# Differential mixer: each normalized output is transposed five steps behind its scores in place of four

## The reference

```
for blk in range(8):                       # 128 queries each, chunk-causal
    sc = einsum('bqhmd,bkhmd->bhmqk', q[blk], k[:qe]) * 64**-0.5   # 4 heads, 2 maps m
    sc = where(allowed, sc + bias, NEG_INF)
    pr = softmax(sc)
    a  = pr[:, :, 0] - lam * pr[:, :, 1]
    outs.append(einsum('bhqk,bkhe->bqhe', a, v[:qe]))              # 128 wide
o = rms_norm(concat(outs), subln_g) * (1 - lambda_init)
h = h + concat([oa, ob]) @ w_out           # oa: the sliding-window mixer
```

## Time and profile before

| | us |
|---|---|
| median of 3 runs | 1261.01 |
| lowest, highest | 1259.12, 1261.21 |
| the profiled execution | 1262.01 |
| its span | 1259.9 |
| PE busy in the span | 1219.5 |

### The profile page before, as it was taken

The page is one execution under the profiler, slowest core; times in us unless marked ns, Lnnn a source line. Parts: engine busy times, 40 slices in busy tenths (PEclk is TensorE's granted clock), DMA queues, the critical chain, the costliest instruction groups (busy, mean ns, idle before and its releaser), DMA issues.

```text
span 1259.9 us, 17110 instructions
## 1 busy us (share of the span) xinstructions
PE 1219.5 (97%) x6167; PEld 1004.0 (80%) x6167; DVE 868.3 (69%) x1510; ACT 517.3 (41%) x1042; POOL 248.5 (20%) x291
## 2 busy tenths in 40 slices
PE   8999999999789999999999999999999999999997
PEld 7997787887667787888888888888888888888885
DVE  5423786777886466887787777877677898964442
ACT  4311664665664224433333333333344444643321
POOL 0000000354454122232323323223120000000000
PEclk9999999999899999999999999999999999999998
DMA  7464233112833411333332323223398533620101
GB/s 210 91 89 87 51 85 84 31 43 72 219 124 61 141 50 59 101 110 99 112 98 85 125 88 122 84 84 125 135 326 317 174 94 104 222 67 25 43 34 50
DMA packets 128668, 136.07 MB, mean 108 GB/s; under 512 B 15570, under 2 KB 93130, under 8 KB 128522
## 3 DMA queue, kind: packets, MB, share of 16 engines
q1 hardware_dynamic: 128586, 135.00, 35.6%
HBM read 96.77 MB, written 37.22 MB: 106 GB/s over the span
## 4 chain that ended last, share of the span: by engine, by line
PE 63%; issue 2%; DVE 2%; DMA 1%; SPq 0%; ACT 0%; POOL 0%; POOLq 0%; DVEq 0%
PE ps L1687 62%; PE ps L1693 1%; DMA act_t<-mix_a 1%; DVE xs L1453 0%; PE ps L1927 0%; DVE h L1448 0%; DVE conv L1392 0%; SPq L479 0%; POOL stat L678 0%; ACT xs L787 0%; DVE act_t L1167 0%; PE ps L2077 0%; DVE gel L1680 0%; DVE h L1669 0%; DVE conv L1666 0%
## 5 line engine op out<-in xcount | busy, mean ns | idle before, releaser
L1687 PE MATMUL ps<-act_t,wbuf 128*128 128x512 f32 x1200 | 290.0, 398 | 2.9 <-DVE wbuf L1167 2.9
L1687 PEld LDWEIGHTS ps<-act_t,wbuf 128*128 128x128 f32 x1200 | 226.7, 189 | 57.8 <-issue 3.3
L1687 PE MATMUL ps<-wbuf 128*128 128x512 f32 x912 | 215.5, 391 | 0.0
L1687 PEld LDWEIGHTS ps<-wbuf 128*128 128x128 f32 x912 | 170.6, 188 | 36.2
L1687 PE MATMUL ps<-act_t,wq 128*128 128x512 f32 x624 | 155.7, 402 | 3.6 <-DVE wq L1169 2.8
L1687 PEld LDWEIGHTS ps<-act_t,wq 128*128 128x128 f32 x624 | 114.6, 188 | 33.5 <-issue 7.4
L678 POOL TENSOR_TENSOR stat<-stat 128x1 f32<-128x1 f32 x32 | 17.6, 549 | 437.9 <-DVE stat L1176 437.9
L784 ACT ACTIVATE wbuf<-raw 128x512 fp32r<-128x512 f32 (+1 forms) x107 | 69.0, 647 | 79.4 <-PE ps L1687 65.4
L1167 DVE TENSOR_TENSOR wbuf<-raw,wbuf 128x512 fp32r<-128x512 f32 (+1 forms) x107 | 87.6, 819 | 13.4 <-ACT wbuf L784 13.1
L1687 PE MATMUL ps<-hx,wbuf 128*128 128x512 f32 x408 | 96.2, 391 | 0.0
L1687 PEld LDWEIGHTS ps<-hx,wbuf 128*128 128x128 f32 x408 | 76.5, 188 | 16.6
(11 more groups left out here) (203 smaller groups left out, 2003.5 us busy)
## 6 DMA issues: line engine op xcount, KB each, us to landing
u_ops<-wbuf_f SPq DMA_DIRECT2D x77, 256.0 KB, 2.2
raw<-u_ops SPq DMA_DIRECT2D x77, 256.0 KB, 2.8
raw<-in_w_ffn_in SPq DMA_DIRECT2D x33, 512.0 KB, 3.9
g_ffn<-in_w_ffn_in SPq DMA_DIRECT2D x11, 512.0 KB, 4.1
act_f<-in_w_ffn_out SPq DMA_DIRECT2D x21, 256.0 KB, 3.7
w_raw<-in_w_in SPq DMA_DIRECT2D x10, 512.0 KB, 4.7
wbuf_f<-in_w_ffn_out SPq DMA_DIRECT2D x18, 256.0 KB, 6.7
x_in<-in_x SPq DMA_DIRECT2D x8, 512.0 KB, 3.8
```

The costliest lines, as they stand in the source:

```text
L1687: return nc.tensor.matmul(dst, lhs, rhs, start=start, stop=stop)
```

## The change

y of a block is turned in step m+5 in place of m+4 (in the steps n % 8 == 1 the two are blocks n-6 and n-5 in place of n-5 and n-4). ACT and DVE get one step more at the end for the last y. On PE the y turned right behind the last c_units is now that of block 29, ahead of the first piece of `oproj`; blocks 30 and 31 follow at the two places where 30 and 31 stood.

```
         if n % NT == 0:
             return ()
-        ms = (n - 5, n - 4) if n % NT == 1 else (n - 4,)
+        ms = (n - 6, n - 5) if n % NT == 1 else (n - 5,)
         return tuple(m for m in ms if 0 <= m < NBS)
...
-        for n in range(NBS + 5):
+        for n in range(NBS + 6):
...
         for c in c_units(NBS + 2):
             c_unit(c)
+        y_turn(NBS + 2)
         pe.wait_ge(S.mix_45, 16 * 4)
         pe.wait_ge(S.b_exp, 2 * NBS)
         oproj(1, O_ROWS[:2])
-        y_turn(NBS + 2)
+        y_turn(NBS + 3)
         pe.wait_ge(S.c_added, 2 * NT)
         oproj(0, O_ROWS[:2])
-        y_turn(NBS + 3)
+        y_turn(NBS + 4)
         pe.wait_ge(S.b_ylo, 3 * NT)
```

## The result

| | before | after |
|---|---|---|
| median of 5 runs each, us | 1259.93 (1259.12 to 1261.21) | 1267.38 (1265.63 to 1269.37) |
| ratio, 95% interval | | 1.0049 [1.0027, 1.0071] |
| profiled execution, us | 1262.01 | 1269.37 |
| span, us; granted clock | 1259.9; 0.990 | 1267.3; 0.987 |

The change makes the kernel slower by 7.4 us, by the medians (7.45) as by the two profiled executions (7.36). The forecast was 7.3. The ratio, taken from the same runs, stands for 6.2 us and its interval for 3.4 to 8.9, so the time alone does not tell 7.3 from 5 or 8; the terms are told apart only in the traces.

The account below looks back on a forecast made before the run. PE, busy 97% of the span, was taken to bound the kernel, with SP's queue on its path in step 22. Terms: 0 + 5.2 + 2.1 + 0 = +7.3 us, so 1268.3 us for the median; range 1264.5 to 1271.5.

Parts of the forecast that it names:

- What bounds: PE bounds, busy 97% of the span; in step 22 its path goes through SP's queue, behind step 23 DVE and ACT bound.
- SP's queue: Step 22: the later store of block 15's y delays the reads back, and so c_unit(0); cost 5.2 us, at least 3.8.
- Waits of PE for y: Between 300 and 412 us, 3.8 us of PE's waits for POOL go, but other waits follow; value 0, bounds 0 and -1.3.
- 6 to 7 foreseen: Sign expected in the changed kernel's profile: PE idle for 6 to 7 us before the first c_unit.
- The clock: PE's longer gap in step 22 brings a stretch at the lower clock; cost 2.1 us, bounds 0 and 5.1.
- the low clock from the start: Rival, chance 10%: all 5.1 us of PE's work from c_unit(0) through the scores of step 23 at half rate, 1271.3 us.
- POOL's buffers: Steps 9, 17, 25, 33: two y buffers hold POOL, making ACT 0.7 us late; cost 0, bounds 0 and 0.7 in first three.
- that rival: Rival, chance 8%: POOL's hold is not absorbed at the heads, 3 x 0.7 = 2.1 us more, 1270.4 us.
- Loads behind a store, and the end: Loads behind moved stores still come in time, and the later last y hides in the mixer's end wait; cost 0.
- no change: Rival, chance 7%: reads back shift but most is hidden by shorter landing and DVE's bound; +2.5 us at the least, 1263.5.

Follow-up runs that it names:

- e1: Kernel before, with SP waiting for the low part of one more y block before the reads back; 1267.34 us, ratio 1.0054 to before.
- e2: Changed kernel, with the sliding-window mixer's reads back issued before the stores of the y of blocks 14 and 15; 1258.94 us, ratio 0.9996 to before.
- e4: Changed kernel, with 27 added matmuls on PE between the scores of step 22 and the wait for the reads back; 1268.18 us, ratio 1.0056 to before.
- e6: Changed kernel, with three y buffers in place of two; 1265.9 us, ratio 1.0045 to before.
- e8: Kernel before, with reads back ahead of the last store, and output projection row 7 ahead of rows 2 and 3, its load early; 1255.22 us, ratio 0.9966.
- e9: Changed kernel, with reads back before the last two stores, output projection row 7 and its load earlier, and three y buffers; 1254.91 us, ratio 0.9963.
- e5: Changed kernel, with 36 added matmuls on PE in the gap before the reads back have landed; 1266.31 us, ratio 1.0043 to before.
- e7: Changed kernel, with reads back before the last two stores, and output projection row 7 before rows 2 and 3, its load early; 1253.5 us, ratio 0.9945.
- e3: Kernel before, with the sliding-window mixer's reads back issued before the store of the y of block 15; 1260.39 us, ratio 0.9995 to before.

## Why the prediction was right

**What bounds.** That c_unit(0) is set by SP's queue was read from "issue", a sum of two times, and the lack of an engine as releaser. e1 and e2 show it from both sides: one wait more on SP gives the whole loss, and the reads ahead of it take it away. The sum of the two times fits wherever PE waited there: last issue plus longest landing gives 338.4 in e1 (c_unit(0) began at 338.47), 337.8 in e4 (337.82) and 335.1 in e6 (335.16).

**Waits of PE for y, 0 us.** The 3.8 us went and came back as waits for the low part of y (1.5 us) and as longer waits for the exponentials (2.1 us): 1.15 became 1.54 us in step 20, and the wait in step 28 grew from 0.98 to 1.51 us. What was won ahead of step 22 only made the gap there longer: the scores of step 22 ended 0.74 us earlier behind the landmark, and PE then stood idle for 7.61 us, more than the 6 to 7 foreseen. e8 and e9, with the waits and without, take the same time within their intervals. The value was right, and of the bound of -1.3 us nothing came.

**SP's queue, 5.2 us.** Counted from the landmark, the reads started 327.57 - 299.58 = 27.99 us behind it against 22.79 before, 5.20 us later, and c_unit(0) 5.37 us later, a little above the 5.2 given as the most, since the longest read took 7.2 us to land and not 6.9. The step that took this from the order of DVE's low parts held.

**The clock, 2.1 us.** In the changed kernel's trace it measured 2.78 us (6.20 - 3.42), and e5 gives 2.75, so against these two it was too small, within its bounds of 0 and 5.1. But it is not one size: e1 and e6 have the like gap, with the clock low from the first matmul too (it fell at 336.2 in e1 and at 332.4 in e6, ahead of c_unit(0)), and take 5.57 and 5.35 us from c_unit(0) to the scores of step 23, so there it was 2.15 and 1.93 us. The forecast's 2.1 lies inside what four executions show, and the 0.7 us that it missed here are no more than their spread. The reason given, one stretch as behind the gap before `mix_23`, was wrong in kind, though the forecast allowed that the low level "may be there already". There PE had resumed at the full level for 1.4 us; here the clock had fallen in the gap, so the low level met the path from its first matmul. So the mechanism of the rival "the low clock from the start", which had 10%, is the one that came, and only its price was too high; that the total fell on the forecast all the same is in part luck. The rival doubled 5.1 us, the scores of step 23 among them; these began as the clock came back, so only the 3.42 us ahead of them were concerned. The Trainium skill (TensorE: Matmul & The Clock Gate, HAM oscillation) says that the burst behind such a wait starts cold. The trace of step 22 agrees, that of the earlier trace rows does not.

**The wait in SP's queue against the issue time.** e1 changes nothing but what SP waits for, and costs 0.54%. The Trainium skill (DMA: Bandwidth & Descriptors, Issuing engines are not separate DMA queues) says that issuing on several engines saves only the issue time. That does not cover a wait at the head of the queue.

**POOL's buffers, 0 us.** In step 9, y of block 5 was complete at 263.01 (forecast 262.7) and ACT's square came at 263.63 (forecast 263.5), with a wait of 0.50 us for POOL. The wait behind it, 0.71 us in the earlier trace rows, was gone, and ACT's copy there came at 264.48 against 264.22, no later than PE's transposes of the step (262.12 against 261.86). So the hold was absorbed, as foreseen.

```profile
262.55 0.46 POOL L703 TENSOR_TENSOR bias_a<-o_t,g_sub 128x128 f32<-128x128 f32 x1 [3.49 <-PE ps L1860]
...
263.63 0.31 ACT L787 ACTIVATE bias_a<-o_t 128x128 f32<-128x128 f32 x1 [0.50 <-POOL o_t L694]
...
264.48 0.28 ACT L784 ACTIVATE a_t<-ps 128x128 fp32r<-128x128 f32 x1
```

In step 25, where DVE and ACT bound and not PE, 0.24 us were not absorbed (e6). That is inside the bounds, a third of the price of that rival at one of its three places.

**Loads behind a store, and the end: 0 us.** The load behind the first store was issued at 241.79 and its first use came at 253.86, against 253.61, which is the 0.25 us by which the landmark moved. At the end, the copy of the last row waited 9.74 us and not 6.99, so the last y was complete at 424.2; PE went through its 54 matmuls without a gap.

**The errors against each other.** Terms left out, 0.7 us of clock and 0.3 us between the scores of step 24 and "resume", and 0.4 us ahead of c_unit(0) or of the landmark, were paid back by 1.3 us behind the mixer. What gave it back can be read in the trace. Both kernels wait 2.9 us there for a `wbuf`, and the 12 matmuls behind that wait took 4.32 us before and 3.04 after, a difference of 1.3 us: the granted clock fell at 491.8 in the kernel before, ahead of them, and in the changed one it stayed at the full level. First the kernel before, then the changed one, then e1.

```profile
492.42 4.32 PE L1687 MATMUL ps<-act_t,wbuf 128*128 128x512 f32 x12 [2.90 <-DVE wbuf L1167]
```

```profile
501.12 3.04 PE L1687 MATMUL ps<-act_t,wbuf 128*128 128x512 f32 x12 [2.90 <-DVE wbuf L1167]
```

```profile
501.01 5.46 PE L1688 MATMUL ps<-act_t,wbuf 128*128 128x512 f32 x12 [2.90 <-DVE wbuf L1168]
```

The same 12 matmuls behind the same wait take 3.03 to 3.04 us in the changed kernel, e8 and e9, 4.19 to 4.44 in the kernel before, e2, e5, e6 and e7, and 5.46 in e1, e3 and e4. So they go neither with the change nor with any edit: e8 and e9 have y at different places and agree, e6 and the changed kernel have it at the same place and differ. No step of the forecast speaks of it. That the terms left out were paid back to 0.1 us is luck; by its terms the forecast was right to about 1.5 us. Two of its bounds do not quite follow from its own sums: the low clock from the start comes to 1271.3 and the range ends at 1271.5, and the least cost that the rival "no change" works out, 2.5 us, leaves out the 1.7 us of clock that the lower end of the range counts. Neither touches the forecast.

## What to carry to other kernels

A wait at the head of an in-order queue delays everything behind it, also what does not depend on it: when a producer is moved, list what stands behind its store on the issuing engine, and put ahead of it what does not need it (here this decided 7 us, and on the engines whose work was moved no more than 0.24 us was found). A wait "for issue" that ends at the last DMA's issue plus its landing time is a wait for that DMA. When waits are taken away, ask for each what else would have ended it: 3.8 us of waits were worth under 1 us between e2 and e3 and nothing that can be seen between e8 and e9.

## What the runs showed of the hardware

The same eight reads do not take the same time in each execution. From the first issue for `mix_23` to PE's first matmul behind them it was 11.7 to 12.1 us in the kernel before, the changed one, e2, e5 and e6, and 13.3 to 13.8 in e1, e3, e4 and e7 to e9. The longest landing was 6.9 to 7.1 us in the first group and 8.4 to 8.9 in the second, but for e4, where it was 7.5 and the eight issues took 6.84 us in place of 5.74. The edits of e1, e3 and e4 do not touch these reads, so their 1.3 us or so are most likely the execution's; no kernel was traced twice, so this was not shown. In e7 to e9 one more load stands ahead of the reads.

The stretch ahead of the landmark varied too: 299.58 us in the changed kernel and 295.36 in e2, whose code is the same up to there. That is more than most terms of a sum like this one; only differences from the landmark tell 0.2 us apart.

A gap does not fix how the clock stands when PE resumes, nor whether it falls. Behind 3.54 us of idle time it was at the full level for 1.4 us more, and behind 3.24 us in the changed kernel for about 0.2 us. Behind 3.25 us in e2 it had fallen 0.7 us before PE resumed. The views are of the changed kernel and of e2.

```profile
420.50:421.00 0.50, 0.41 (x2) 0.81 1.01 401
...
424.00:424.50 0.50, 0.50 (x3) 0.78 0.00 0
```

```profile
406.50:407.00 0.50, 0.00 (x0) 0.66 0.93 254
```

Behind 7.61 us, in the changed kernel, it had been low for 4.3 us. In e4 it fell 1.1 us after PE resumed, behind 2.58 us of idle time. The gap of 2.90 us above, the same in all 11 traces, left the 12 matmuls behind it at 3.0, 4.2 to 4.4 or 5.5 us. So what one gap costs in the clock can't be read from its length here, and a single trace gives the term only to 1 or 2 us.
